# Packing the first four experts of each router through token rows and transposes

## The reference

```python
def ec_moe(h, w_r, w1, w3, w2):
    B, n, D = h.shape
    cap = max(1, EC_CAPACITY * n // N_EXPERTS)
    aff = jax.nn.softmax((h @ w_r).astype(jnp.float32), axis=-1)
    gate, idx = lax.top_k(jnp.swapaxes(aff, 1, 2), cap)
    xin = jax.vmap(lambda hb, ib: hb[ib])(h, idx)
    hid = jax.nn.silu(jnp.einsum('becd,edf->becf', xin, w1)) * jnp.einsum('becd,edf->becf', xin, w3)
    ye = jnp.einsum('becf,efd->becd', hid, w2) * gate[..., None].astype(h.dtype)
    return jax.vmap(lambda yb, ib: jnp.zeros((n, D), h.dtype).at[ib.reshape(-1)].add(yb.reshape(-1, D)))(ye, idx)
...
        h2 = modulate(rmsnorm(x, g_norm2[i]), sh2, sc2)
        x = x + gt2 * ec_moe(h2, w_router[i], w_e1[i], w_e3[i], w_e2[i])
        if not last:
            h2c = modulate(rmsnorm(xc, g_norm2[i]), sh2c, sc2c)
            xc = xc + gt2c * ec_moe(h2c, w_router[i], w_e1[i], w_e3[i], w_e2[i])
```

## Time and profile before

| | |
|---|---|
| median of 3 runs | 2851.66 us (2849.84 to 2852.05) |
| the profiled execution | 2853.2 us, of which the span from the first to the last instruction is 2850.9 us |
| PE busy | 2604.5 us, 91% of the span |
| DVE busy | 811.9 us, 28% |
| ACT busy | 445.9 us, 16% |
| mean TensorE clock granted | 0.956 of full speed |
| weights and data moved | 664.28 MB, 233 GB/s on average |

### The profile page before, as it was taken

The page is one execution under the profiler, slowest core; times in us unless marked ns, Lnnn a source line. Parts: engine busy times, 40 slices in busy tenths (PEclk is TensorE's granted clock), DMA queues, the critical chain, the costliest instruction groups (busy, mean ns, idle before and its releaser), DMA issues.

```text
span 2850.9 us, 30941 instructions
## 1 busy us (share of the span) xinstructions
PE 2604.5 (91%) x13317; PEld 1551.7 (54%) x13317; DVE 811.9 (28%) x1768; ACT 445.9 (16%) x1000; POOL 60.7 (2%) x91
## 2 busy tenths in 40 slices
PE   8999999999999999999999998987999998666665
PEld 5678888578883444444444442333556786332322
DVE  2535511435502553333112121112334412110101
ACT  1320010130002022121111111103111311000001
POOL 1010000000000100000000000000100000000000
PEclk9999999999999999999999999999999999777777
DMA  8676453464444310212338999999622368999997
GB/s 300 218 196 167 164 169 129 163 230 159 155 159 138 111 59 30 74 56 78 150 122 350 415 421 421 421 421 393 197 69 79 119 227 339 421 421 421 420 421 315
DMA packets 202971, 664.28 MB, mean 233 GB/s; under 512 B 14226, under 2 KB 60596, under 8 KB 153940
## 3 DMA queue, kind: packets, MB, share of 16 engines
q1 hardware_dynamic: 193952, 641.97, 58.8%
q0 software_dynamic: 8688, 20.28, 2.8%
q10 hardware_dynamic: 196, 0.06, 0.0%
HBM read 661.12 MB, written 9.57 MB: 235 GB/s over the span
## 4 chain that ended last, share of the span: by engine, by line
PE 74%; DMA 20%; DVE 3%; ACT 2%; issue 1%; ACTq 0%; DVEq 0%
PE ps L519 41%; DMA ring<-in_w_e 20%; PE ps L1150 8%; PE ps L540 8%; PE ps L700 5%; PE ps L1127 1%; PE ps L1100 1%; PE ps L635 1%; PE ps L954 1%; PE ps L976 1%; PE ps L909 1%; PE ps L922 1%; PE ps L897 1%; PE ps L651 1%; PE ps L566 0%
## 5 line engine op out<-in xcount | busy, mean ns | idle before, releaser
L519 PE MATMUL ps<-normed,ring 128*128 128x256 f32 (+1 forms) x3456 | 945.2, 434 | 9.7 <-ACT normed L2068 6.6
L519 PEld LDWEIGHTS ps<-normed,ring 128*128 128x128 f32 x3456 | 655.7, 191 | 276.3 <-issue 200.1
L1150 PE MATMUL ps<-ring,arena 128*32 128x256 f32 (+1 forms) x4344 | 588.6, 527 | 180.6 <-DMA ring<-in_w_e 172.5
L1150 PEld LDWEIGHTS ps<-ring,arena 128*32 128x32 f32 (+1 forms) x4344 | 194.1, 133 | 554.9 <-DMA ring<-in_w_e 264.1
L519 PE MATMUL ps<-arena,ring 128*128 128x256 f32 (+1 forms) x832 | 254.0, 462 | 1.3 <-DVE small L1276 1.3
L540 PE MATMUL ps<-ring,normed 128*128 128x512 f32 x512 | 222.8, 593 | 0.0
L519 PEld LDWEIGHTS ps<-arena,ring 128*128 128x128 f32 x832 | 156.1, 190 | 88.1 <-issue 73.1
L1357 DVE COPY arena<-ps 128x256 f32<-128x256 f32 (+1 forms) x102 | 55.6, 553 | 406.9 <-PE ps L519 165.6
L540 PEld LDWEIGHTS ps<-ring,normed 128*128 128x128 f32 x512 | 96.2, 190 | 117.0 <-issue 116.9
L700 PE MATMUL ps<-arena,ring 128*128 128x256 f32 x704 | 152.3, 379 | 0.0
L700 PEld LDWEIGHTS ps<-arena,ring 128*128 128x128 f32 x704 | 133.8, 190 | 18.2
(11 more groups left out here) (261 smaller groups left out, 1798.8 us busy)
## 6 DMA issues: line engine op xcount, KB each, us to landing
ring<-in_w_e SPq DMA_DIRECT2D x363, 1024.0 KB, 20.3
ring<-in_w_in SPq DMA_DIRECT2D x56, 1024.0 KB, 7.4
ring<-in_w_ada SPq DMA_DIRECT2D x48, 1024.0 KB, 7.5
ring<-in_ffn_w_up SPq DMA_DIRECT2D x88, 512.0 KB, 6.3
ring<-in_ffn_w_down SPq DMA_DIRECT2D x22, 1024.0 KB, 5.6
ring<-in_dil_w_qkv SPq DMA_DIRECT2D x18, 1024.0 KB, 5.2
arena<-in_w_e SPq DMA_DIRECT2D x16, 1024.0 KB, 10.2
ring<-in_sb_w_qkv SPq DMA_DIRECT2D x12, 1024.0 KB, 14.9
```

What stands on the lines that cost most here:

```text
L519: ins = mm(o[:, 0:n], slots[k // 4][:, k % 4, f * P:(f + 1) * P], src[:, k, 0:n], start=k == 0, stop=k == kts - 1)
L1150: ins = mm(o[w * g:w * g + w, 0:cols], lhs(2 * c + j), part, start=c == 0 and j == 0, stop=c == KT // 2 - 1 and j == 1)
```

## The change

The first pack of each router is gathered in another orientation. `gather_first` multiplies `SEL0` (stationary) with the token rows `HT` (moving, 512 features), so that the packed tokens come out as rows: two banks per stream, each of 2 matmuls (one per token block). ACT copies the left half of the features, DVE the right half, into `ROWS0`. PE then turns each 128 x 128 block back with a transpose, four per bank, and the modulation is applied on the way out of that second bank: ACT does the four blocks of the left half, DVE the four of the right half. Packs 1 to 3 are gathered as before. On DVE the selection for packs 1 to 3 (`pick(j, (1, 2, 3))`) is moved behind the first pack's copies.

```diff
+        ROWS0 = (view(18432, D), view(20480, D))
...
+                def gather_first():
+
+                    copied = []
+                    for q in range(qtiles // 2):
+                        for half, who in enumerate(("a", "v")):
+                            o = banks.open(who)
+                            pe.wait_ge(*banks.due)
+                            for j in range(ST):
+                                ins = mm(o, SEL0[:, j, q].rearrange("p e s -> p (e s)"), HT[:, ST * q + j, half * 512:(half + 1) * 512],
+                                         start=j == 0, stop=j == ST - 1)
+                            ins.then_inc(banks.filled, 1)
+                            copied.append(read_by(who))
+                    for q in range(qtiles // 2):
+                        for half, who in enumerate(("a", "v")):
+                            o = banks.open(who)
+                            pe.wait_ge(*banks.due)
+                            pe.wait_ge(banks.freed[who], copied[2 * q + half])
+                            turned = ROWS0[q][:, half * 512:(half + 1) * 512].rearrange("p (c m j) -> p c j m", m=P, j=2)
+                            for n in range(4):
+                                ins = nc.tensor.transpose(o[:, n * P:(n + 1) * P], turned[:, n // 2, n % 2, :], ident)
+                            ins.then_inc(banks.filled, 1)
+                    pe.wait_ge(banks.freed["a"], read_by("a"))
+                    pack_in[0] = read_by("v")
...
-                gather(0)
+                gather_first()
...
-                for j in range(ST):
-                    ins = pick(j, (1, 2, 3))
-                ins.then_inc(v_step.sem, v_step.up())
-                v.wait_ge(v_step.sem, v_step.made)
...
-                pack_copies(0)
+                for q in range(ns):
+                    o = banks.take("v")
+                    v.wait_ge(banks.filled, banks.at["v"])
+                    ve.tensor_copy(ROWS0[q][:, 512:D], o).then_inc(banks.freed["v"], banks.free("v"))
+                for q in range(ns):
+                    o = banks.take("v")
+                    v.wait_ge(banks.filled, banks.at["v"])
+                    for n in range(4):
+                        c, j = 2 + n // 2, n % 2
+                        ins = ve.tensor_scalar(XINS[i][0][:, 4 + n, :, q * CAP:(q + 1) * CAP],
+                                               o[:, n * P:(n + 1) * P].rearrange("p (e s) -> p e s", s=CAP),
+                                               MOD2P[:, c, j, q:q + 1], MOD2P[:, c, j, 2 + q:3 + q], ALU.mult, ALU.add)
+                    ins.then_inc(banks.freed["v"], banks.free("v"))
+                for j in range(ST):
+                    ins = pick(j, (1, 2, 3))
+                ins.then_inc(v_step.sem, v_step.up())
+                v.wait_ge(v_step.sem, v_step.made)
...
                 table(EXP_TANH)
+                for q in range(ns):
+                    o = banks.take("a")
+                    sc.wait_ge(banks.filled, banks.at["a"])
+                    se.activation(ROWS0[q][:, 0:512], o, ACT.Copy).then_inc(banks.freed["a"], banks.free("a"))
+                for q in range(ns):
+                    o = banks.take("a")
+                    sc.wait_ge(banks.filled, banks.at["a"])
+                    for n in range(4):
+                        c, j = n // 2, n % 2
+                        ins = se.activation(XINS[i][0][:, n, :, q * CAP:(q + 1) * CAP],
+                                            o[:, n * P:(n + 1) * P].rearrange("p (e s) -> p e s", s=CAP),
+                                            ACT.Identity, bias=MOD2P[:, c, j, 2 + q:3 + q], scale=MOD2P[:, c, j, q:q + 1])
+                    ins.then_inc(banks.freed["a"], banks.free("a"))
```

More of the change, by code:

```diff
@@ L1100, in gather @@
                                     ins = mm(o[:, n * P:(n + 1) * P], HTP[:, ST * q + j, k // 2, k % 2, :],
-                                             (SELS[i][:, j, e0:e0 + 4] if pk else SEL0[:, j, q]).rearrange("p e s -> p (e s)"),
+                                             SELS[i][:, j, e0:e0 + 4].rearrange("p e s -> p (e s)"),
                                              start=j == 0, stop=j == ST - 1)
```

## The result

| | before | after |
|---|---|---|
| median of 20 runs, on the same chip | 2851.55 us | 2856.65 us |
| span of runs | 2849.76 to 2855.04 | 2853.78 to 2859.63 |
| profiled execution, its span | 2853.2, 2850.9 | 2853.78, 2852.0 |
| busy: PE, DVE, ACT | 2604.5, 811.9, 445.9 us | 2606.1, 810.9, 453.2 us |

The ratio is 1.0016 with a 95% interval of 1.001 to 1.0023: 2.9 to 6.6 us slower (the means differ by 4.6 +/- 1.0). The bound of 0.2% is not reached, so by the measure named in the prediction it is no change, but twenty runs of each tell it from zero. The forecast of +2.8 lies just under the interval; the measured time lies within the range. The profiled execution of the changed kernel was a quick one, 2.9 us under its own median, so its span alone tells little of the difference.

The account below looks back on a forecast made before the run. PE's dense products and the weight stream were taken to set the time, with no cover between gather and expert 0. Losses of 1.7 and 1.1 us added 2.8 to the 2851.66 median: 2854.5 us, range 2851.0 to 2857.5.

Parts of the forecast that it names:

- dear transposes: Price check on PE's transposes: at 0.185 us each throughout, 1.0 us is added in the first layer.
- The chain from the last gather matmul to expert 0, over which no cover lies: At both routers: DMA stands idle, so delaying expert 0's first matmul moves each layer's end 1 to 1.
- Tail in the first layer: Behind the first layer's gather: 16 transposes (1.97 us), then DVE's groups; expert 0 starts 1.7 us later.
- Tail in the second layer: Behind the second gather: DVE copy 0.69, four transposes 0.74, DVE group 1.38, hand-overs; a loss of 1.1 us.
- ACT's half: ACT's modulation of turned blocks: 0.38 us each, ending at 1522.7, just under DVE's 1522.9, in the first layer.
- The rival of 0.75: ACT binds: at 0.75 us an instruction, 2.7 and 0.6 us more in the layers, 2857.8; chance 6%.
- Gather, a gain of 0.7 and 0.4: First and second layers' first-pack gather: wide matmuls, 9% cheaper at full clock, end 0.7 and 0.4 us earlier.
- The sign that the gather ends within 1 us of 1519: First layer: the gather as 16 records ends within 1 us of 1519, counted from 1509.4.
- Selection moved behind, cost 0: DVE's selection for packs 1 to 3, 3.2 us in the first layer, fits before expert 0's hidden product.
- Rival, clock low when the experts begin: PE at half clock from the transposes into expert 0: 4.7 us on top of 2.8, 2859.2; chance 7%.
- The row I named against this rival: Second router, before: PE did nothing in 2386 to 2388, yet the clock was still 1.00.
- Rival, clock rises earlier with wide matmuls: Fewer weight-load gaps at the gathers; at the extreme 2.8 and 1.7 us less, 2850.0; chance 9%.

Follow-up runs that it names:

- the pairs with the clock held: Before, changed kernel and gather by halves, each with spare matmuls at both routers and near the end: -6.6, -3.3 and -9.2 us against before.
- the repeated run: The changed kernel measured once more, unchanged, against before: ratio 1.0018, mean +5.1 +/- 1.0 us.
- The delayed kernel: Before with 12 more DVE instructions per layer, results unused, holding back expert 0: ratio 1.0039, mean +11.3 +/- 1.0 us.
- the two with end fillers: Before and the changed kernel with spare matmuls only near the program's end: ratios to before 0.9998 (-0.4 us) and 1.0014 (+4.2 us).
- the halves: Before with its own gather ordered by feature halves, expert 0 starting on the first half: ratio 0.9993, mean -1.3 +/- 1.1 us.
- each layer alone: The new gather in one layer, the old in the other, against before: first alone 1.0003 (+0.7 us), second alone 1.0001 (+0.8 us).
- before with ACT's small instructions: Before with 12 one-element ACT instructions per layer behind the table load: ratio 1.0001, mean +0.1 +/- 1.2 us.

## Why the prediction was right, and what it missed

The path was right: the time is lost between the gather and expert 0. The size was not. The means differ by 4.6 where 2.8 was forecast; about 0.6 of that is the gather, mis-sized below, and the 1.2 above it has no term in the sum. That the time still lies in the range is in part luck: its upper end was set by dear ACT instructions and dear transposes, which did not come, and it took in something else.

*The chain from the last gather matmul to expert 0, over which no cover lies:* right. The DMA share stayed near 0.00 longer (0.03 in 1523 to 1525), and the pairs with the clock held agree with 1 to 1 (3.3 +/- 0.9 for 2.9, -2.7 +/- 1.2 for -3.05).

*Tail in the first layer, 3.8 from the end of the gather to expert 0:* right; 3.73 (12.27 - 8.54; in the repeated run 13.73 - 10.00). The transposes took 2.07 for 1.97 and DVE's two groups 2.64 for 2.76.

*Tail in the second layer, 2.94:* 3.10 (8.52 - 5.42), 0.16 dearer, mostly in the hand-overs.

*ACT's half, 0.38 an instruction, between 0.297 and 0.474:* 2.91 / 8 = 0.364. It ends 0.2 ahead of DVE in the first layer and does not bind in the second. The rival of 0.75 is out.

*Gather, a gain of 0.7 and 0.4:* **the term that was mis-sized.** It gave 0.38 (10.00 against 10.38 at the same clock) and 0.12 (5.42 against 5.54). I took the end of the old gather as measured, but priced the new one by its pace alone, 0.429 a record. At full clock (the chains with fillers) its 16 records take 7.13 where the pace gives 6.87, and the old 64 take 7.82 where 64 x 0.118 gives 7.55: both have 0.26 to 0.27 more than their pace, and only the old end had it in my sum. The same sum with the rise at 2.9 us gives 8.32 for the gather of the result's profile, and it took 8.54. The shortfalls (0.3 and 0.3), the 0.16 above and 0.07 less in the first tail turn 2.8 into the 3.4 to 3.5 that the distances show.

The 9% itself holds only at full clock: there the wide form saves 0.69 (7.82 - 7.13) and 0.34 (3.86 - 3.52). The 5.8 us at half clock lengthened the old gather by 2.6 (10.38 against 7.82) and the new one by 2.9 (10.00 against 7.13), so in that stretch the narrow records lost less, and little of the gain was left. That my 0.7 is the saving at full clock is chance.

The sign that the gather ends within 1 us of 1519 (9.6 after its start) failed in the result's profile: it took 8.54, because the clock rose at 2.9. In the repeated run it took 10.00.

*Selection moved behind, cost 0:* not contradicted. With it moved back the mean is +4.3 +/- 1.3, against +5.1 +/- 1.0 and +4.6 +/- 1.0 as it was.

*Rival, clock low when the experts begin:* it did not happen in any profile of the changed kernel. PEclk stayed 1.00 through 16 transposes and 1.8 us of idle PE behind them. The delayed kernel shows that the mechanism is real when PE idles 5.3 us. By the Trainium skill, TensorE: Matmul & The Clock Gate, "Part 4: PE-mode transpose", transposes do not count as PE-busy in the same way as matmuls. The trace neither refutes nor needs this: transposes and idle time together were 3.9 us, and in the delayed kernel, with no transposes, PE stopped at 1519.6 and 1.00 held until about 1524.0. The row I named against this rival was weak: in before's idle stretch at 2386 to 2388 the clock was 1.00, but it fell at about 2389.0, some 4.8 us after PE had stopped.

*Rival, clock rises earlier with wide matmuls:* it rose at 2.9 us once and at 5.8 in the repeated run of the same kernel. In all, the profiles with the new gather in the first layer show 2.9, 3.4, 3.4, 5.8 and 5.8, those with the old one 3.0, 3.5, 3.5, 5.8, 5.8 and 5.8. So the width doesn't decide it, and the moment of the rise doesn't explain why the changed kernel is slower. Distance follows it at about half: 13.73 at 5.8, 12.54 at 3.4, 12.27 at 2.9.

**What stays open.** The four plain comparisons (+4.6, +5.1, +4.3, and +4.6 between the two with end fillers) each have an error of 1 or more. Weighted by their errors they give 4.7 +/- 0.6, about 1.3 above 3.4, so together they put the excess clear of zero. The time of a run also holds 2.20 us outside the span in before and 1.81 in the changed kernel (means of 27 and 11 runs of the repeated comparison). From the first instruction to the last the change therefore costs 0.4 more, 5.5 +/- 1.0 there and 3.6 +/- 0.9 with the clock held at the routers. No run shows what the 0.4 is.

The profiles point to a place for the excess: behind the second layer's expert 0. From its first matmul to the end of the span before takes 451.5 us, each layer alone 451.2 and 451.4, before with ACT's small instructions 451.6, but the changed kernel 453.4, the repeated run 453.9 and the one with the selection moved back 453.8 (the halves 452.9). The second layer alone issues the same instructions there as the changed kernel and is not longer. (Between the first layer's expert 0 and the second gather the profiles of either kernel differ by some 4 us among themselves, 867.6 to 871.2 and 867.7 to 871.8, so that stretch tells nothing.) Most of the 2 to 2.5 us is the last scatter. It is a row in the chain at the end of the program; first before's, then that of the changed kernel:

```profile
2837.55 3.72 PE ps L1127 x16
```

```profile
2836.90 5.41 PE ps L1152 x16
```

In before, in each layer alone and with ACT's small instructions it ran at full clock; in the result, the repeated run, the selection moved back, the delayed kernel and the halves it ran at half for a part (5.15 to 5.41, 1.4 to 1.7 longer). The window of the result's profile there, PEclk 0.50:

```profile
2838.00:2840.00 2.00, 2.00 (x6) 1.64 (x5) 1.25 (x3) 0.15 (x1) 0.00 (x0) 0.50 0.00 0
```

The other 0.3 to 0.9 us lie ahead of the last scatter. With the fillers in, where both last scatters took 3.72, the changed kernel still had 452.4 against 451.5, and PEclk was 0.83 in 2820 to 2830 against 1.00.

Moving the whole program's end by 3 us could shift it into a low stretch more often; it could also be why each layer alone cost less than its chain and why halves gained less than theirs. But the profiles are single executions, the experiment to hold the clock there failed, and the comparison with the clock held (3.3 +/- 0.9) doesn't exclude a true cost of 4. This is an association, not a shown cause.

## What to carry to other kernels

Where a full ring of weights waits for the first consumer, find the chain between last producer and first consumer: there a microsecond is a microsecond, and a cheaper producer is no gain if what it adds behind itself (here a copy, a transpose and a hand-over) is longer than what it saves. Shorten such a chain by letting the consumer begin on the part that is ready, and give an idle PE spare matmuls if its clock is low just afterwards. Compare two profiles only over distances that had the clock at the same level.

## What the runs showed that I had not expected

The same instructions in the same order had the clock rise 2.9 us after the gather's start in one execution and 5.8 in the next, worth 1.5 us of distance (12.27 and 13.73). Two profiles of one kernel can differ by more than the change under study.

Spare matmuls at the routers were worth more than any rearrangement of the gather: PEclk 1.00 in place of a low stretch, 6.6 +/- 1.1 us in all, for work whose results nobody reads. The same kind of filler near the end, alone, gave nothing that can be told (-0.4 +/- 1.2 in before), and in the changed kernel it did not keep the clock up (0.50 through 2830 to 2834).
